# A gated linear recurrence beside attention and a large projection: both column tiles' decay distances in one instruction per level

## The reference

```
h = rmsnorm(x, g_pre) * (1 + scale) + shift          # scale, shift, gate from c @ w_ada + b_ada
p = h @ w_in                                         # 8704 columns, split among four mixers and their gates
y_pool, y_hgrn, y_conv, y_diff = mixers of p, each times the SiLU of its gate columns
merged = sum over the mixers of sigmoid(gate columns) * (y @ w_merge)
x = x + gate * rmsnorm(merged @ w_out, g_post)
```

```
scores[t, s] = sum_k q[t, k] * exp(b[t, k] - b[s, k]) * k[s, k]     for s <= t
o = (q * exp(b)) @ S + scores @ v
S = exp(b_last) * S + (k * exp(b_last - b))^T @ v
```

## Time and profile before

| | |
|---|---|
| median of the three timed runs | 2533.78 us |
| the profiled execution, and its span | 2534.88 us, 2533.1 us |
| TensorE (PE) busy, of the span | 2274.4 us, 90% |
| VectorE (DVE) | 1434.6 us, 57% |
| ScalarE (ACT) | 1144.1 us, 45% |
| GpSimd (POOL) | 839.4 us, 33% |

### The profile page before, as it was taken

The page is one execution under the profiler, slowest core; times in us unless marked ns, Lnnn a source line. Parts: engine busy times, 40 slices in busy tenths (PEclk is TensorE's granted clock), DMA queues, the critical chain, the costliest instruction groups (busy, mean ns, idle before and its releaser), DMA issues. The chain is left out here.

```text
span 2533.1 us, 35157 instructions
## 1 busy us (share of the span) xinstructions
PE 2274.4 (90%) x11572; PEld 1871.5 (74%) x11572; DVE 1434.6 (57%) x2638; ACT 1144.1 (45%) x2400; POOL 839.4 (33%) x739
## 2 busy tenths in 40 slices
PE   3698799998999889898999999999999966989898
PEld 2486677777777668687888888878888844767676
DVE  5676566655888777312766666445556334444442
ACT  3553455543544543422666666434434233434341
POOL 0113223223745645200222222124343225244353
PEclk7799999999999989999999999999999988999999
DMA  6799777757767667989464654588777676576581
GB/s 227 260 352 328 259 231 241 223 204 277 264 239 261 230 222 253 332 265 264 163 191 146 181 169 149 171 258 250 230 247 235 213 238 178 155 190 187 148 226 61
DMA packets 383963, 564.75 MB, mean 223 GB/s; under 512 B 32432, under 2 KB 248880, under 8 KB 382768
## 3 DMA queue, kind: packets, MB, share of 16 engines
q1 hardware_dynamic: 315248, 313.01, 42.0%
q10 hardware_dynamic: 68544, 249.59, 27.8%
HBM read 331.28 MB, written 231.21 MB: 222 GB/s over the span
## 5 line engine op out<-in xcount | busy, mean ns | idle before, releaser
L1682 PE MATMUL gb<-h_hi,w_both 128*128 128x512 f32 x1904 | 789.0, 414 | 87.2 <-ACT o L949 41.7
L1684 PE MATMUL gb<-h_hi,w_both 128*128 128x512 f32 x1904 | 757.7, 398 | 0.0
L1683 PE MATMUL gb<-h_lo,w_both 128*128 128x512 f32 x1904 | 756.7, 397 | 0.0
L1682 PEld LDWEIGHTS gb<-h_hi,w_both 128*128 128x128 f32 x1904 | 366.9, 193 | 171.2 <-issue 91.7
L1684 PEld LDWEIGHTS gb<-h_hi,w_both 128*128 128x128 f32 x1904 | 365.7, 192 | 81.2
L1683 PEld LDWEIGHTS gb<-h_lo,w_both 128*128 128x128 f32 x1904 | 367.7, 193 | 67.1
L949 ACT ACTIVATE o<-gb 128x512 f32<-128x512 f32 x272 | 161.4, 594 | 372.5 <-PE gb L1684 308.0
L809 POOL TENSOR_TENSOR C_prob<-C_prob,C_cf 128x512 f32<-128x512 f32 (+3 forms) x160 | 156.9, 1005 | 506.1 <-DVE C_cf L1358 492.1
L1014 ACT ACTIVATE C_prob<-C_sc,C_negm 128x512 f32<-128x512 f32 (+3 forms) x320 | 198.5, 622 | 246.6 <-DVE C_negm L1336 239.9
L1250 DVE TENSOR_TENSOR o<-gb,o 128x512 f32<-128x512 f32 x204 | 140.3, 688 | 231.0 <-PE gb L1684 220.0
L1240 DVE TENSOR_TENSOR w_both<-w,w_both 128x512 fp32r<-128x512 f32 x170 | 142.1, 836 | 171.5 <-ACT w_both L922 171.1
(11 more groups left out here) (230 smaller groups left out, 3722.6 us busy)
## 6 DMA issues: line engine op xcount, KB each, us to landing
wS_scratch<-w_both ACTq DMA_DIRECT2D x238, 512.0 KB, 4.4
w_both<-wS_scratch ACTq DMA_DIRECT2D x238, 512.0 KB, 4.3
w<-in_w_in_dram SPq DMA_DIRECT2D x68, 512.0 KB, 5.2
gT_scratch<-o SPq DMA_DIRECT2D x128, 256.0 KB, 4.6
D_gate<-gT_scratch SPq DMA_DIRECT2D x32, 1024.0 KB, 9.8
pT_scratch<-o SPq DMA_DIRECT2D x80, 256.0 KB, 4.2
C_qt<-qB_scratch SPq DMA_DIRECT2D x128, 128.0 KB, 3.4
C_ks<-kT_scratch SPq DMA_DIRECT2D x48, 256.0 KB, 5.7
```

Source lines behind the costliest of these rows:

```text
L1682: mm(to, hi[:, k, :], h_hi[j][:, k, :], start=(fresh and k == 0), stop=False, skip_group_check=True)
L1683: mm(to, hi[:, k, :], h_lo[j][:, k, :], start=False, stop=False, skip_group_check=True)
L1684: last = mm(to, lo[:, k, :], h_hi[j][:, k, :], start=False, stop=(k == KH - 1), skip_group_check=True)
```

## The change

The seven distances of a block are taken for both column tiles in one instruction each (128 rows by 2 x 128 columns), and one spread covers both tiles. Four of the levels stand at offset -5 and three with the spread at -4; before, tile 0 stood at -7 and -6 and tile 1 at -3 and -2. `decay_keys` moves from -5 to -6, the first queries from -4 to -2, the first keys from -3 to -1. ScalarE's two exponentials stand at -3 both; they were at -5 and -1. The distances wait for all four score rounds of the block before.

```diff
@@ -1091,7 +1091,7 @@
                 ins.then_inc(decayed, 1)
 
             def level_decays(i, t):
-                act.wait_ge(spread, 2 * i + t + 1)
+                act.wait_ge(spread, i + 1)
                 a(X[:, t, 0:NL - 1, :], X[:, t, 0:NL - 1, :], ACT.Exp).then_inc(xready, 1)
 
             def query_decays(i):
@@ -1211,7 +1211,7 @@
                 i = mix_step(n, -7)
                 if i is not None:
                     key_decays(i)
-                for t, off in enumerate((-5, -1)):
+                for t, off in enumerate((-3, -3)):
                     i = mix_step(n, off)
                     if i is not None:
                         level_decays(i, t)
@@ -1405,19 +1405,20 @@
                                                   f_s[:, :, :].rearrange("p n t -> p (n t)"), 0.0, ALU.mult, ALU.add))
                 nc.vector.tensor_copy(f_s[:, 0, 0:1], b_s[:, 0, 0:1]).then_inc(scanned, 1)
 
-            def distances_x(i, t, y0, y1):
+            def distances_x(i, y0, y1):
+
                 dve.wait_ge(scanned, i + 1)
                 if i:
-                    dve.wait_ge(r_done, 4 * (i - 1) + 2 * t + 2)
+                    dve.wait_ge(r_done, 4 * i)
                 for y in range(y0, y1):
                     m = LEVELS[y]
-                    v = b_s[:, t, :].rearrange("p (n u) -> p n u", u=2 * m)
-                    to = X[:, t, y, :].rearrange("p (n u) -> p n u", u=2 * m)
-                    ins = tt(to, v, v[:, :, m - 1:m].to_broadcast([P, P // (2 * m), 2 * m]), ALU.subtract)
+                    v = b_s[:, :, :].rearrange("p t (n u) -> p t n u", u=2 * m)
+                    to = X[:, :, y, :].rearrange("p t (n u) -> p t n u", u=2 * m)
+                    ins = tt(to, v, v[:, :, :, m - 1:m].to_broadcast([P, 2, P // (2 * m), 2 * m]), ALU.subtract)
                 link(ins)
                 if y1 < NL - 1:
                     return
-                flat = X[:, t, 0:NL - 1, :]
+                flat = X[:, :, 0:NL - 1, :]
                 stt(flat, flat, -1.0, flat, ALU.mult, ALU.min).then_inc(spread, 1)
 
             def decay_keys(i):
@@ -1617,25 +1618,21 @@
                 i = mix_step(n, -8)
                 if i is not None:
                     scan(i)
-                i = mix_step(n, -7)
-                if i is not None:
-                    distances_x(i, 0, 0, 3)
                 i = mix_step(n, -6)
                 if i is not None:
-                    distances_x(i, 0, 3, NL - 1)
+                    decay_keys(i)
                 i = mix_step(n, -5)
                 if i is not None:
-                    decay_keys(i)
+                    distances_x(i, 0, 4)
                 i = mix_step(n, -4)
                 if i is not None:
+                    distances_x(i, 4, NL - 1)
+                i = mix_step(n, -2)
+                if i is not None:
                     decay_first_queries(i)
-                i = mix_step(n, -3)
+                i = mix_step(n, -1)
                 if i is not None:
                     decay_first_keys(i)
-                    distances_x(i, 1, 0, 2)
-                i = mix_step(n, -2)
-                if i is not None:
-                    distances_x(i, 1, 2, NL - 1)
                 i = mix_step(n, 11)
                 if i is not None:
                     advance_state(i)
```

## The result

| | before | after |
|---|---|---|
| median (20 runs each on one chip) | 2534.83 us (2527.38 to 2543.06) | 2541.14 us (2536.30 to 2549.89) |
| ratio, with its 95% interval | | 1.0027 (1.0019 to 1.0036) |
| profiled execution, span | 2534.88, 2533.1 us | 2545.57, 2543.8 us |

The changed kernel is slower, by 6.3 us of the medians, and outside the range given. The two profiled executions lie 10.7 us apart in span, somewhat more than the medians.

A forecast was written before the change was run, and what follows sets the result against it. The prediction took TensorE's first-pass waits for VectorE's additions and ScalarE's copies as the bound. Savings of 5.6 + 4 = 9.6 us idle, times 1.57, gave 15 us: 2519 us on the median's scale, with an 8-in-10 range of 2502 to 2534.

The forecast's parts named there:

- What bounds the kernel: First pass of mixer blocks: 48.7 us lost there, 31.1 of it TensorE idle; none lost in the second pass.
- The instructions: VectorE's distances and spread: wide ones take 0.422 and 2.03 us, saving 1.19 us per block, 19 us in 16 blocks.
- Where the distances go: Five and four products ahead of the first scores: distances meet an idle GpSimd and run near 0.42 us.
- What leaves the last three products: VectorE's queue before the first scores: small distances and a spread go, saving 5.6 us of TensorE idle time.
- What moves with it: Earlier second exponential and GpSimd decays: ScalarE's wait for the state update falls 7.7 us, TensorE idle time 4 us.
- New waits: First scores wait for first keys one product ahead: 2.7 us of slack, costed at nothing.
- The rule that the prediction weighs: SBUF access: a two-input VectorE instruction and a GpSimd instruction reading SBUF exclude each other for a whole instruction.
- the first keys come late: Rival, chance 0.10: GpSimd's decays hold queries and keys, keys 4.25 us late, 20 us idle, 16 us slower, 2550.
- the signs named as showing the forecast wrong: In the profile: scores waiting for VectorE's first keys, queries near 2 us, or waits for ScalarE's copy unchanged.
- The table loads decide: Rival, chance 0.15: time saved at first scores is waited again two products later at ScalarE; at most 2 us, 2531.
- The factor: First pass: each microsecond of TensorE idle time costs 1.57 us, from 48.7 us lost over 31.1 idle.

The follow-up runs named there:

- the narrow forms: Changed kernel with one distance and one spread instruction per column tile again: ratio 1.0037; the same with first queries three and first keys two products ahead: 0.9973.
- the keys early: Changed kernel with first queries three and first keys two products ahead of the first scores, instead of two and one: 2523.17 us, ratio 0.9960.
- the state update's move: Changed kernel with queries at three, keys at two products ahead, and the state update ten products behind its base instead of eleven: 2521.25 us, ratio 0.9956.

## Why the prediction was wrong, step by step

**What bounds the kernel** held: the second pass did not move, and all of the difference lies in the first pass of blocks.

**The instructions** came out as sized (418 and 2025 ns), and are worth about nothing in the end, which the narrow forms show. **Where the distances go** held too: 474 ns on average beside GpSimd in the first pass, against 501 for half the columns in the earlier trace rows.

**What leaves the last three products** was real: TensorE's waits for VectorE's addition fell by 10.9 us, more than the 5.6 costed, and by 9.9 with the keys early. **What moves with it** was only half so. GpSimd's wait for the exponential went, but ScalarE's wait for the state update rose from 15.4 to 27.1 us, since the update itself now comes behind the late keys (with the keys early it is 12.9). The fall of the wait for ScalarE's copy (13.3 to 5.5) cannot be put down to an earlier start of the table loads, since ScalarE comes to them later; more likely the scores now wait where the bank wait used to stand. The run with only the queries and keys moved bears this out: its exponentials are the old ones, its scores wait 16.0 us, and its wait for the copy is 6.5 us. With the keys early it fell to 9.6, which is close to the 4 us of that term.

**New waits** is the step that failed: "2.7 us of slack, and I cost it at nothing". The slack was reckoned from VectorE's own durations, 0.68 + 0.89 + 1.09 us, as though nothing held them and its queue never stood still. The rule that the prediction weighs puts the queries and keys beside GpSimd's work, and the prediction priced this in a rival and left it out of the sum. The runs showed a hold of 3.4 to 4.9 us on queries, low part and keys in the six blocks whose scores wait, more than the whole slack, and with GpSimd's decays behind the keys five of the six waits are gone.

Block 2 has a second cause. Product 153 starts at about 724.3 there and the keys end at 732.9, 8.6 us later instead of 2.7: the addition starts 1.2 late behind held queries, the low part waits 2.70 for ScalarE, and the keys are held for 1.9, with 0.2 more on the low part. Of 5.4 us allowed that is 3.2 too many, and TensorE stood 3.08. The wait of the low part was there to be read. The earlier trace rows give the low parts 49.3 us of idle time ahead of them, 49.1 of it for ScalarE's rounding, and the trace of before has that rounding waiting for GpSimd's weight sum in the same block 2. Here are ScalarE's rounding and VectorE's low part, of before:

```profile
722.96 0.63 ACT L922 ACTIVATE w_both<-s 128x512 fp32r<-128x512 f32 x1 [5.31 <-POOL s L788]
```

```profile
725.66 0.68 DVE L1240 TENSOR_TENSOR w_both<-s,w_both 128x512 fp32r<-128x512 f32 x1
```

ScalarE's wait ended at 722.96, and VectorE did not notice it, since five distances and a spread kept it busy until 725.06. The change took that cover away and put the keys behind the wait that came out. The lost cover is not what decides over all blocks, though: with only the queries and keys moved the distances still stand there, and the scores wait as long.

**The rival "the first keys come late"** is what happened, and its price in idle time was close: 20 us forecast, 21.3 measured (14.8 at the scores in six blocks, 6.5 more at the norms). Its mechanism was right in the main and its size, keys 4.25 us late, lies among the 3.4 to 4.9 us of the holds, but in part by luck: the holds on queries and keys average 1.2 and 1.4 us (2.32 and 2.51 against 1.09), not a whole GpSimd instruction, and the rest is the hold on the low part between them and, in block 2, that low part's wait. It had neither. Its total of +16 us was too high because what stood against it was 18.7 us of bank waits and not 9.6. Its chance of 0.10 was too low: the argument against it, that a hold of two whole instructions needs GpSimd to win each time, left out the low part between them. Of the signs named as showing the forecast wrong, the first two came: score matmuls that wait for the first keys, and queries of 2.3 us.

**The table loads decide** holds in part once the keys are early: the state update's move was given back at the banks. **The factor** of 1.57 us for each idle microsecond is not a constant: the early keys save 14.2 us of the periods for 7.1 us of idle time, a factor of 2.0, and after lost 6.9 us for 0.6. In both the rest is TensorE's own busy time, 297.8 and 311.2 us against 304.9, at a mean granted clock of 0.97 and 0.93 against 0.94.

The forecast's sum of 15 us was thus near that of a kernel with the keys where they do no harm: 321 us were forecast for the seven periods, and the early keys have 321.8. That this is so close is partly luck, 9.6 us of idle time at 1.57 against 7.1 at 2.0, and the whole execution gained 10.7 us there (2533.91 to 2523.17, on its chip).

## What to carry to other kernels

Slack on an in-order queue is not the sum of the durations that stand ahead: for the moved instruction and each one that it will stand behind, read which work of another engine will lie beside it and how long it takes there, what it waits for, and what covers that wait today. A price that is argued for a rival belongs in the sum too, at least as a part. Work that leaves a queue uncovers the waits of what stays (block 2), so a value that another engine needs soon should stand ahead of an instruction that waits for a third engine, not behind it. Where two multiplications of two engines hold each other, putting one behind the other only moves the hold to whatever stands next in that queue.

## What the runs showed of the hardware

The hold goes both ways. A multiplication of 128x896 takes 1.09 us alone on VectorE and up to 3.02 beside GpSimd's decay products, a low part 0.69 us alone and up to 2.60 beside them, and the first of GpSimd's products grows from a median of 2.127 to 2.569 us (L856). With GpSimd's products behind VectorE's keys that median is 2.117 us again (L857; 2.126 at most), and the keys' is 1.081. The Trainium skill (SBUF — State Buffer, section Who interferes with whom) has issue order decide who blocks, and so either engine can be the one delayed; the trace agrees, with 1.09 to 3.02 us on the one and 2.13 to 2.57 us on the other.
